# A decoder layer on one core: early sums of the first down chunk, later squares, and a new order of the last additions

## The reference

```python
x = x + cross_attention(rmsnorm(x, g_cross), rmsnorm(mem, g_mem), w_xq, w_xkv, w_xo)
u = rmsnorm(x, g_mlp) @ w_up                      # 1024 -> 4096
x = x + jnp.square(jax.nn.relu(u)) @ w_down       # 4096 -> 1024
return rmsnorm(x, g_final)                        # x * rsqrt(mean(x*x) + 1e-6) * g
```

## Time and profile before

| | us |
|---|---|
| median of 3 runs | 424.05 (423.93 to 424.34) |
| profiled execution | 423.02 |
| its span, first to last instruction | 420.9 |
| PE busy | 409.4 (97%) |
| DVE busy | 335.8 (80%) |
| ACT busy | 250.8 (60%) |
| POOL busy | 27.5 (7%) |

### The profile page before, as it was taken

The page is one execution under the profiler, slowest core; times in us unless marked ns, Lnnn a source line. Parts: engine busy times, 40 slices in busy tenths (PEclk is TensorE's granted clock), DMA queues, the critical chain, the costliest instruction groups (busy, mean ns, idle before and its releaser), DMA issues.

```text
span 420.9 us, 7064 instructions
## 1 busy us (share of the span) xinstructions
PE 409.4 (97%) x2839; PEld 376.5 (89%) x2839; DVE 335.8 (80%) x446; ACT 250.8 (60%) x300; POOL 27.5 (7%) x39
## 2 busy tenths in 40 slices
PE   8999999999999999999999999999999999999992
PEld 8999978999999999889988898899999999999971
DVE  6587566967757437875856899999999999999976
ACT  7664228773665634652556368877777777776723
POOL 0079200000000000000200000000000000000002
PEclk9999999999999999999999999999999999999998
DMA  8999545433234255555352345466555555554002
GB/s 297 421 416 379 199 188 182 154 145 123 101 112 188 101 201 200 201 186 179 135 202 100 106 176 178 153 213 208 204 202 208 202 207 205 201 206 183 2 0 100
DMA packets 12539, 77.47 MB, mean 184 GB/s; under 512 B 1376, under 2 KB 1376, under 8 KB 4064
## 3 DMA queue, kind: packets, MB, share of 16 engines
q1 hardware_dynamic: 12512, 77.09, 50.7%
HBM read 76.04 MB, written 1.05 MB: 183 GB/s over the span
## 4 chain that ended last, share of the span: by engine, by line
PE 88%; DVE 6%; ACT 2%; issue 2%; DMA 1%; POOL 0%; POOLq 0%; DVEq 0%; ACTq 0%
PE bank L1114 39%; PE bank L1133 16%; PE bank L1380 15%; PE bank L1228 11%; PE bank L1240 1%; DVE res L1045 1%; PE bank L1326 1%; DVE t_lo L683 1%; PE bank L1346 1%; DVE t_sum L940 1%; DVE f_lo L683 1%; PE bank L1147 1%; DMA head_all<-in_head_dram 1%; PE bank L1269 1%; DVE w_lo L683 1%
## 5 line engine op out<-in xcount | busy, mean ns | idle before, releaser
L683 DVE TENSOR_TENSOR w_lo<-raw,w_hi 128x2048 fp32r<-128x2048 f32 (+2 forms) x87 | 147.9, 1708 | 26.4 <-ACT w_hi L435 25.4
L1114 PE MATMUL bank<-hT_hi,w_hi 128*128 128x256 f32 x416 | 117.2, 282 | 0.7 <-DVE hT_lo L695 0.4
L1114 PE MATMUL bank<-hT_hi,w_lo 128*128 128x256 f32 x416 | 116.7, 281 | 0.0
L1114 PE MATMUL bank<-hT_lo,w_hi 128*128 128x256 f32 x416 | 116.3, 280 | 0.0
L1114 PEld LDWEIGHTS bank<-hT_hi,w_hi 128*128 128x128 f32 x416 | 78.3, 188 | 1.9 <-issue 0.6
L435 ACT ACTIVATE w_hi<-raw 128x2048 fp32r<-128x2048 f32 x33 | 62.8, 1914 | 27.3 <-PE bank L1114 13.8
L1114 PEld LDWEIGHTS bank<-hT_lo,w_hi 128*128 128x128 f32 x416 | 78.3, 188 | 0.6
L1114 PEld LDWEIGHTS bank<-hT_hi,w_lo 128*128 128x128 f32 x416 | 78.2, 188 | 0.0
L1228 PE MATMUL bank<-hT_hi,w_hi 128*128 128x256 f32 x128 | 36.8, 288 | 0.0
L683 DVE TENSOR_TENSOR t_lo<-t_sum,t_hi 128x1024 fp32r<-128x1024 f32 x30 | 36.5, 1218 | 0.0
L1228 PE MATMUL bank<-hT_hi,w_lo 128*128 128x256 f32 x128 | 36.0, 282 | 0.0
(11 more groups left out here) (195 smaller groups left out, 823.4 us busy)
## 6 DMA issues: line engine op xcount, KB each, us to landing
raw<-in_weights_dram SPq DMA_DIRECT2D x65, 1024.0 KB, 4.8
head_all<-in_head_dram SPq DMA_DIRECT2D x7, 256.0 KB, 4.0
raw<-in_chunk_dram SPq DMA_DIRECT2D x4, 256.0 KB, 5.0
raw<-in_chunk_dram SPq DMA_DIRECT2D x2, 512.0 KB, 6.5
res<-in_x_dram SPq DMA_DIRECT2D x2, 512.0 KB, 11.3
mem_tok<-in_mem_dram SPq DMA_DIRECT2D x1, 1024.0 KB, 12.1
memT_raw<-in_memT_dram SPq DMA_DIRECT2D x1, 1024.0 KB, 10.9
out_dram<-xs SPq DMA_DIRECT2D x2, 512.0 KB, 2.7
```

The lines of the kernel that those rows point to most:

```text
L683: return nc.vector.tensor_tensor(dst, whole, high.bitcast(fp32), sub)
L1114: last = mm(outs[m], w, v[:, k0 + k, :], start=first and n == 0, stop=k == nk - 1 and n == 2, skip_group_check=bool(kt_wait))
```

## The change

Three things. First, DVE's three sums of down chunk 0 are made in the cross attention: `sum_t13(0)` ahead of the `x_pT` copies, `sum_t2(0)` behind them, `sum_t4(0)` ahead of the second `aT_lo`; ACT's two `t_hi` copies of it come ahead of its part of the transposes. Behind `low_T` DVE does the `lo` parts of chunk 0, then `sum_t13(1)`, the forms, `sum_t2(1)`, `f_lo(0)` and the rest of pair 1. Second, ACT's squares of the residual and DVE's three steps to `rstd` and `neg_rstd` move from the middle of the MLP to its end. Third, at the end `f_lo` of the last pair goes ahead of `v_form` and the first `add_p`; the `gain` instructions between the x3 go; POOL adds the half means and epsilon in one instruction and multiplies one half with its gain; and one DVE instruction (`finish`) scales and multiplies with the gain in one.

```diff
@@ sync
-                sp.wait_ge(fin, t + 1)
+                sp.wait_ge(fin, t + 2)
@@ gpsimd, the end
-            for t in range(TOK):
-                pool.wait_ge(sumsq_act, 2 * t + 2)
-                nc.gpsimd.tensor_scalar(x3_part[:, t:t + 1], x3_ms[:, t, 0:1], EPS, 0.0, ALU.add, ALU.add)\
-                    .then_inc(x3_parted, 1)
-                pool.wait_ge(x3_mean, t + 1)
+            def x3_rstd(t):
+                pool.wait_ge(sumsq_act, 2 * t + 3)
+                step(nc.gpsimd.tensor_scalar(var[:, X3, t:t + 1], x3_ms[:, t, 1:2], x3_ms[:, t, 0:1], EPS, ALU.add,
+                                             ALU.add))
                 nc.gpsimd.tensor_tensor(rstd[:, X3, t:t + 1], var[:, X3, t:t + 1], half[:, 0:1], ALU.pow)\
                     .then_inc(rstd_ready, 1)
+            pool.wait_ge(gfin_in, 16)
+            pool.wait_ge(x3_ready, 1)
+            nc.gpsimd.tensor_tensor(xs[:, 0, 0:512], res[:, 0, 0:512], gfin[:, 0:512], ALU.mult).then_inc(pool_gained, 1)
+            x3_rstd(0)
+            x3_rstd(1)
@@ scalar
             high_down(0)
+            high_t13(0)
+            high_t24(0)
             for k in range(KT):
                 high_T(X2, k, hT_hi, G_MLP)
-            high_t13(0)
-            high_t24(0)
...
             mlp_step(1)
-            act.wait_ge(x2_ready, TOK)
-            for t in range(TOK):
-                copy(xs[:, t, :], res[:, t, :], ACT.Square, accum_out=stat[:, X2, t:t + 1]).then_inc(x2_sumsq, 1)
...
             high_forms(u)
+            act.wait_ge(x2_ready, TOK)
+            for t in range(TOK):
+                copy(xs[:, t, :], res[:, t, :], ACT.Square, accum_out=stat[:, X2, t:t + 1]).then_inc(x2_sumsq, 1)
             square_relu(u + 1)
...
-                act.wait_ge(x3_parted, t + 1)
-                act.wait_ge(sumsq_act, 2 * t + 3)
-                copy(var[:, X3, t:t + 1], x3_ms[:, t, 1:2], ACT.Identity, bias=x3_part[:, t:t + 1]).then_inc(x3_mean, 1)
-            act.wait_ge(gained, 4)
+            act.wait_ge(gained, 1)
             act.wait_ge(rstd_ready, 5)
-            copy(xs[:, 1, D // 2:D], xs[:, 1, D // 2:D], ACT.Copy, scale=rstd[:, X3, 1:2]).then_inc(fin_act, 1)
+            copy(xs[:, 1, 0:512], xs[:, 1, 0:512], ACT.Copy, scale=rstd[:, X3, 1:2]).then_inc(fin_act, 1)
@@ vector, cross attention
+            sum_t13(0)
             for h in range(XH):
                 dve.wait_ge(x_t, h + 1)
                 nc.vector.tensor_copy(x_pT[:, h, :], bank[X_PT[h]][:, :]).then_inc(x_pt, 1)
+            sum_t2(0)
             for p in range(2):
+                if p == 1:
+                    sum_t4(0)
                 dve.wait_ge(xo_hi, p + 1)
@@ vector, start of the MLP
-            sum_t13(0)
-            sum_t2(0)
-            sum_t4(0)
             low_down(0, B11, B22 + 1, 2)
             low_t13(0)
+            low_down(0, B21, B21 + 1, 3)
+            low_t24(0)
+            sum_t13(1)
             form_s31(0)
             form_s2(0)
             form_s4(0)
-            low_down(0, B21, B21 + 1, 3)
-            low_t24(0)
+            sum_t2(1)
             low_forms(0)
-            mlp_step(1)
+            mlp_rest(1)
@@ vector, the end (the three steps to rstd move behind low_down of the last pair)
                 .then_inc(s_made, 1)
+            low_forms(u, upto=6)
...
             add_p(1, 0, p1_copy[:, :], r2)
-            low_forms(u, upto=6)
...
             x3(0, 0)
-            gain(0, 0)
             x3(0, 1)
             add_p(1, 1, bank[P5][:, :], r2).then_inc(v_made, 1)
             x3(1, 0)
-            gain(0, 1)
             dve.wait_ge(v_made, 5)
             x3(1, 1)
-            normed(0, slice(0, D))
-            gain(1, 0)
-            gain(1, 1)
-            normed(1, slice(0, D // 2))
+            def finish(t, c):
+                cols = slice(512 * c, 512 * c + 512)
+                dve.wait_ge(x3_ready, 2 * t + c + 1)
+                dve.wait_ge(rstd_ready, 4 + t)
+                nc.vector.scalar_tensor_tensor(xs[:, t, cols], res[:, t, cols], rstd[:, X3, t:t + 1], gfin[:, cols],
+                                               ALU.mult, ALU.mult).then_inc(fin, 1)
+            finish(0, 1)
+            dve.wait_ge(pool_gained, 1)
+            nc.vector.tensor_scalar(xs[:, 0, 0:512], xs[:, 0, 0:512], rstd[:, X3, 0:1], None, ALU.mult).then_inc(fin, 1)
+            dve.wait_ge(x3_ready, 3)
+            nc.vector.tensor_tensor(xs[:, 1, 0:512], res[:, 1, 0:512], gfin[:, 0:512], ALU.mult).then_inc(gained, 1)
+            finish(1, 1)
```

More of the change, by code:

```diff
@@ L238, in hybrid_layer @@
         x3_ms = sb("x3_ms", [P, TOK, 2])
-        x3_part = sb("x3_part", [P, TOK])
         x_scale = sb("x_scale", [P, 2])
@@ L298, in hybrid_layer @@
         tile_done, x3_ready, gained = sem("tile_done"), sem("x3_ready"), sem("gained")
+        pool_gained = sem("pool_gained")
         fin, fin_act = sem("fin"), sem("fin_act")
-        x3_parted, x3_mean = sem("x3_parted"), sem("x3_mean")
         block = ctx.enter_context(nc.Block())
@@ L904, in _ @@
                 last.then_inc(x_normed, 1)
[L905 to L927, removed]
             def blocks(t, n):
@@ L954, in sum_t4, with low_up, low_down @@
                 sum_t(u, T4, B21, T2, 3 * u + 2, i)
+            sum_t13(0)
+            for h in range(XH):
+                dve.wait_ge(x_t, h + 1)
+                nc.vector.tensor_copy(x_pT[:, h, :], bank[X_PT[h]][:, :]).then_inc(x_pt, 1)
+            sum_t2(0)
+            for p in range(2):
+                if p == 1:
+                    sum_t4(0)
+                dve.wait_ge(xo_hi, p + 1)
+                low(aT_lo[:, 2 * p:2 * p + 2, :], bank[p].rearrange("p (b q) -> p b q", b=2),
+                    aT_hi[:, 2 * p:2 * p + 2, :])\
+                    .then_inc(xo_lo, 1)
+            split(35)
+            def low_up(u, i=0):
+                c = up_chunk(u)
+                dve.wait_ge(up_hi, PER * i + (u + 1))
+                low(w_lo[:, c % RAW, :], raw[:, c % RAW, :], w_hi[:, c % RING, :]).then_inc(up_lo, 1)
+            def low_down(u, a, b, made, i=0):
+                c = down_chunk(u)
+                dve.wait_ge(down_hi, PER * i + (u + 1))
+                dve.wait_ge(t_made, 3 * PER * i + made)
+                cols = slice(H * a, H * b)
+                low(w_lo[:, c % RAW, cols], raw[:, c % RAW, cols], w_hi[:, c % RING, cols]).then_inc(down_lo, 1)
             def low_t13(u, i=0):
@@ L995, in mlp_step, with mlp_rest @@
                 sum_t13(u, i)
-                if u > 1:
-                    low_forms(u - 1, i)
+                low_forms(u - 1, i)
                 sum_t2(u, i)
+                mlp_rest(u, i)
+            def mlp_rest(u, i=0):
                 low_up(u + 1, i)
@@ L1028, in _ @@
                     mlp_step(u, i)
-            dve.wait_ge(x2_sumsq, TOK)
-            step(nc.vector.tensor_scalar(var[:, X2, :], stat[:, X2, :], 1.0 / D, EPS, ALU.mult, ALU.add))
-            step(nc.vector.reciprocal(rstd[:, X2, :], var[:, X2, :]))
-            step(nc.vector.tensor_scalar(neg_rstd[:, :], rstd[:, X2, :], -1.0, None, ALU.mult))
             u = PAIRS - 2
@@ L1038, in _ @@
             low_down(u, 2, 4, 3 * u)
+            dve.wait_ge(x2_sumsq, TOK)
+            step(nc.vector.tensor_scalar(var[:, X2, :], stat[:, X2, :], 1.0 / D, EPS, ALU.mult, ALU.add))
+            step(nc.vector.reciprocal(rstd[:, X2, :], var[:, X2, :]))
+            step(nc.vector.tensor_scalar(neg_rstd[:, :], rstd[:, X2, :], -1.0, None, ALU.mult))
             dve.wait_ge(gfin_in, 16)
@@ L1041, in _ @@
             a = blocks(forms[:, :], P)
-            nc.vector.tensor_tensor(a[:, D1:D2 + 1, :], a[:, A11:A12 + 1:2, :], a[:, A21:A22 + 1:2, :], sub)                .then_inc(s_made, 1)
+            nc.vector.tensor_tensor(a[:, D1:D2 + 1, :], a[:, A11:A12 + 1:2, :], a[:, A21:A22 + 1:2, :], sub)\
+                .then_inc(s_made, 1)
+            low_forms(u, upto=6)
             def add_p(t, c, src, scale):
@@ L1063, in x3 @@
                 add_p(t, c, bank[X3_BANKS[2 * t + c]][:, :], r2).then_inc(x3_ready, 1)
-            def gain(t, c):
-                s = slice(512 * c, 512 * c + 512)
-                dve.wait_ge(x3_ready, TOK * t + c + 1)
-                nc.vector.tensor_tensor(xs[:, t, s], res[:, t, s], gfin[:, s], ALU.mult).then_inc(gained, 1)
-            def normed(t, cols):
-                dve.wait_ge(gained, 2 * t + 2)
-                dve.wait_ge(rstd_ready, 4 + t)
-                nc.vector.tensor_scalar(xs[:, t, cols], xs[:, t, cols], rstd[:, X3, t:t + 1], None, ALU.mult)\
-                    .then_inc(fin, 1)
             x3(0, 0)
-            gain(0, 0)
             x3(0, 1)
```

## The result

| | before | after |
|---|---|---|
| median | 423.93 us (423.56 to 424.34, 5 runs) | 420.13 us (419.90 to 420.47, 5 runs) |
| profiled execution | 423.02 | 420.47 |
| its span | 420.9 | 418.7 |
| span, median | 421.7 (19 later runs) | 418.4 (5 runs) |

The ratio is 0.9913 [0.9899, 0.9927]: 3.80 us less, where 3.04 was forecast. The sign, the places and the mechanism came out as predicted. In microseconds the interval of the ratio is 3.1 to 4.3, so the forecast lies just outside it. Most of this study is about the missing 0.8 us.

The account below looks back on a forecast made before the run. PE, 88% of the span, was taken as the bound, with three stalls for `f_lo` and a tail behind its last matmul. 1.49 (MLP start) + 1.55 (tail, last stall included) = 3.04; 424.05 - 3.04 = 421.0 us, range 420.3 to 422.5.

Parts of the forecast that it names:

- The sum: Whole kernel: 1.49 + 1.55 = 3.04 us less, taken from the median 424.05, gives 421.0.
- (a): PE's stall before down(0), 0.30 us waiting for `f_lo`: goes, with 0.13 to spare.
- (b): PE's stall before down(1), 1.05 us: goes; down(1) moves from 266.39 to about 264.90, 1.49 us, nothing to spare.
- Rival 1: MLP start: DVE's chain comes later than reckoned, (b) stays in part; half gives 421.7, all of (a) and (b) 422.5; chance 0.15.
- The squares: ACT's two squares of the residual, 1.04 us each, mid-MLP: gave DVE a wait of 0.1 at most.
- part 2: Squares and three small DVE steps moved to the MLP's end: fit into idle time, cost 0, at worst 0.4 us.
- Part 3: Last pair, `f_lo` first: the 1.03 us stall before `down_plain` goes; x3(1,1) at 412.15 ties with PE's last matmul.
- Part 4: Tail, half means and scalings: `finish(1,1)` ends at 415.56, 415.86 or 416.23 against 417.78; POOL's gain takes 0.8 to 1.4 us.
- rival 2: End: POOL's gain takes 2.5 us, as if held, giving 422.1; chance 0.09.
- the chosen ending: Tail: POOL is held over all three back-to-back DVE instructions, second `rstd` at 415.39, end at 416.23, 1.55 us less.
- ACT's `var` (0.29) goes: Tail: ACT's step goes, with its steps to and from POOL; POOL's one-instruction addition is taken as 0.27 us.
- Rivals 3 and 4: Slower POOL gain ahead of both rstd, 425.6 at 6 us, chance 0.03; early sums uncovered before `x_pT`, 423.6, chance 0.07.

Follow-up runs that it names:

- e3: The kernel before, unchanged, run again under another name as a control and profiled anew: 423.82 us, ratio 1.0001.
- e4: The changed kernel, run again unchanged and timed against before on the same chip: 420.28 us, ratio 0.9916.
- e5: The changed kernel with the squares of the residual and DVE's three steps to rstd back in the middle of the MLP: 420.83 us, ratio 0.9928 to before.
- e1: The kernel before with only the early sums of down chunk 0 and the new order behind `low_T`, squares left in place: 422.67 us, ratio 0.9976.
- e9: The kernel before with one move, `f_lo` of the last pair ahead of `v_form` and the first `add_p`: 423.48 us in one execution.
- e10: The changed kernel without POOL's gain, DVE making that half with a second `finish`: 421.03 us in one execution.
- e6: The kernel before with only POOL adding both half means and epsilon in one instruction: 424.52 us in one execution.
- e12: The changed kernel with one DVE scaling moved to ACT, and ACT adding the half means for tokens 128 to 255: 420.23 us, ratio 0.9918 to before.
- e2: The kernel before with all edits at the last pair and behind it, without the early sums and moved squares: 421.64 us, ratio 0.9947.

## Why the prediction was wrong in size and right in place

**The sum: the step that failed.** "The profiled execution took 423.02 (span 420.9), the median of the runs is 424.05, 1.03 more; 424.05 - 3.04 = 421.0." This takes all that lies outside the reckoned stalls and the tail as unchanged, without a reason: the time outside the span, and what comes ahead of M. The first went from 2.12 to 1.75, for a cause that stays open. The forecast 421.01 is 0.88 above 420.13. Of this 0.37 is that time, and 0.08 (up to 0.16 with e3 and e4) is missing in the sum inside the span. Another 0.12 is the median of before, which was 424.05 in three runs and 423.93 in five. The last 0.3 isn't located; it is no more than the place of M and with it a median of five can shift. The range didn't cover it either: its lower end, 420.3, is the ending in which POOL is never held, not room for such terms. With 3.1 to 3.2 inside and 0.37 outside 3.5 us follow; e4's comparison measured 3.57, and the interval of the first one (3.1 to 4.3) holds 3.5 too.

**(a) and (b).** Forecast 1.49, measured 23.29 - 21.81 = 1.48 at down(1); 0.29 of it is stall (a). The chain of DVE was reckoned as just long enough, and so it was. DVE waits 0.42 for `f_hi` and 0.71 for `w_hi`, which the reckoning had; the next `f_lo` starts at 264.52, 1.31 ahead of down(1), where PE needs 1.23 (e5: 1.24), so less than 0.1 is to spare. Rival 1 didn't occur.

**The squares.** "The two squares [...] gave DVE a wait of 0.1 at most" was true of before and wrong as a price. Behind the early sums they cost 0.42 (e1, e5). The total didn't suffer, since the change moves them; it was right only with part 2 in it, which the text had put at 0.

**Part 3.** `f_lo` to the first x3 was to take (409.96 - 406.38) + 1.27 = 4.85, and took 408.91 - 404.07 = 4.84. The last x3 was forecast in a tie with PE's last matmul; DVE's chain was the one that ended last. (24 at 4.78/21 from 406.45 end at 411.9 and not at 412.1, which changes nothing.) `down_plain`'s 1.03 was counted inside the tail's figure, and e9 shows why it must not be added: alone it is worth 0.4 to 0.5.

**Part 4.** POOL's gain took 1.30 us, within the chosen 0.8 to 1.4; rival 2 didn't occur. DVE's five rows above it (408.91 to 412.32) read one tensor from PSUM and one from SBUF, and POOL wasn't shut out until they ended: its gain was done at 411.11, and the first `var` and power ran beside them in 0.30 and 0.57. The second `var` was held to the end of DVE's three instructions, as the chosen ending says, and ended 0.08 behind them; it lay under two of them, since `finish` was over when it started. The forecast had the last DVE row end 1.55 + 1.49 = 3.04 earlier; it ends at 171.59 behind M instead of 174.68, 3.09. DVE's series itself ended where it was forecast, 170.00 behind M. The 0.05 lies behind it: the power took 0.57 where 0.71 was taken from POOL's other powers (two columns), and the steps before and after it cost 0.09 more.
The Trainium skill (GPSIMD Engine Reference, § 8 Key points) names two SBUF inputs or a 2-port mode as what contends with GpSimd. The traces agree in both directions: held beside the scaling and the gain (0.92 for 0.30) and, in e10, beside `finish` and the gain (1.17), free beside x3. The page doesn't speak of a series; here the hold didn't end between its instructions.
The same page of the Trainium skill (GPSIMD Engine Reference, § 3.1) has 4497 ns for 2048 elements, an estimate of 1.1 us for 512; the trace has 1.30.

**"ACT's `var` (0.29) goes"** was counted as a saving. e6 shows it costs 0.3 to 0.4 us by itself: it trades a step on a free engine for one on an engine that DVE holds. In the full change the rest outweighs it, and e12 measures the other way round that giving it back to ACT brings the last row 0.37 forward.

**Rivals 3 and 4** (slower by POOL's gain, a new wait ahead of `x_pT`): POOL's row is far from 5 us, and `x_pT` starts behind an idle 0.38 (0.3 forecast).

## What to carry to other kernels

Read a stall's price at the place where the work ends, not at the engine that waits: where two limits lie close together (PE before `down_plain`, DVE between the x3), removing one brought 0.4 to 0.6 us where PE alone stood still for 1.0; all edits of the end together (e2) brought 1.7. Keep small GpSimd instructions on the critical path away from stretches in which VectorE runs SBUF-only instructions back to back; what counts is when that series ends, not how many instructions GpSimd has. And before a sum of a few us is set against a median, count from a landmark inside the kernel, and put what varies ahead of it and the time outside the span into the range: here they were some 0.3 and 0.37 us of 3.80.

## What the runs showed of the hardware that was not expected

- GpSimd wasn't let in between back-to-back VectorE instructions that read and write only SBUF: an addition of one element a partition took 0.30 us free, 0.60, 0.92 and 1.17 under series that ended 0.43, 0.84 and 1.0 to 1.1 behind its start, and always ended 0.08 to 0.17 behind the series. A power of the same size took 0.57 free and 1.07 held, and ended 0.43 behind the series.
- The time of a run outside its span is between 1.7 and 2.2 us, steady within 0.13 for one program, and changed by up to 0.4 with edits such as two small fills at the start (1.73 to 2.12); the cause is open.
- The first matmuls on real data can start 0.21 us apart for over 2 us (e3) or 0.12 apart from the second on (before), at a granted clock of 1.00 in both profiles. This and a late piece of input are what the profiles show ahead of M, whose place moved by up to 1.2 us between executions.
- Two output transfers of 512 KB issued within 1.18 us queued behind each other at 404 to 410 GB/s and ended 0.5 us later behind the last compute row than two issued within 1.91.
